# Routed rows of the first expert pair from a one-hot matmul, and the slots of the later pairs moved behind it, in a two-layer decoder trunk

## The chip, the cores and the metric

The kernel runs on one core of one Trainium2 chip. The metric is the device time of one execution in microseconds, as the median of several runs. Engines are called TensorE (PE in the profile, its weight loads PEld), VectorE (DVE), ScalarE (ACT), GpSimd (POOL) and SyncE (SP, which issues the weight DMAs).

## What is computed

A trunk of two layers over 256 tokens of width 1024, with 16 meta tokens ahead of them in layer 0 (272 tokens). Layer 0 has an mLSTM mixer, layer 1 a forgetting attention; each is followed by a mixture of experts, and that is what the change touches:

```python
def hier_moe(h, ...):
    top_g = jnp.argmax(gl, axis=-1)                      # one of 4 groups
    top_v, top_i = lax.top_k(el_g, TOP_K_IN_GROUP)       # 2 of its 4 experts
    p_e = jax.nn.softmax(top_v, axis=-1) * p_g
    gates = (one_hot(eidx, N_EXPERTS) * p_e[..., None]).sum(1)
    for grp in range(N_GROUPS):
        hg = jnp.einsum('td,edf->tef', x, w_gate[sl])
        hu = jnp.einsum('td,edf->tef', x, w_up[sl])
        act = jax.nn.silu(hg) * hu * gates[:, sl, None]
        y = y + jnp.einsum('tef,efd->td', act, w_down[sl])
    return y
```

16 experts of width 256. Everything is float32 but for small exact one-hot and counting matmuls in bf16.

## The kernel before, in words

Each expert has 64 slots (`CAP`), so that a pair of experts has 128, and there are 8 pairs (`NPAIR`). A token takes one slot at each of its two experts. Tokens lie in tiles: two of 128 rows and, in layer 0 only, a third of 16 rows (the meta tokens), `tiles_of(l)`.

*Routing* (`route`, L831 on VectorE). The normed rows of the stream are written by ScalarE to `tok` in SBUF (L575) and from there to `xs` in HBM (L579). VectorE works out groups, experts and, with counting matmuls (L1349), the slots: `tok4[:, 0:2]`, ready at L888. `one_hot` (L893) compares slots with the numbers of 256 slots at a time, in bf16, 12 operations in layer 0 and 8 in layer 1, into `sel`. `rows_of_slots` on TensorE (L1358) multiplies those by token numbers, one column for each block of 128 slots, and `row_of_slot` (L828) turns the result into the indices `idx`. GpSimd gathers with them, from `xs` into one of three buffers `xg` (L454): pair b waits for its part of `idx` and, from the fourth pair on, for the transposes that read the buffer last.

Beside it the weights: VectorE completes `tok4` (L902 to L905), TensorE transposes it (L1367), VectorE copies it to `row4` (L909), TensorE broadcasts its four rows over all partitions (L1371, operand `sel4` of 4 rows), ScalarE copies the result to `bc4` (L600), and `combine_weights` (L931 to L935) makes the combining matrix of a pair from it.

*The loop over pairs.* For each pair TensorE transposes the gathered rows in two halves of four blocks through bank 0 (`rows_to_cols`, L1384), evacuated by VectorE (`x_evac`, L923) and ScalarE (`xgT_evac`, L608); `gate_up(b)` (L1402) multiplies with the gate and up weights of both experts, each operand 64 columns wide, two side by side; silu on ScalarE (L616) and a product on VectorE (`act_mul`, L942) make `ha`; `act_tr` (L1409) transposes it, `down` (L1426) and `combine` (L1441 in layer 0, L1445 in layer 1) finish. The order on TensorE is written out: gate_up(b), [for b = 0: rows_of_slots for pairs 4 to 7], down(b-1), rows_to_cols(b+1, 0), act_tr(b), combine(b-1, 0), rows_to_cols(b+1, 1), combine(b-1, 1). Before the loop stand: rows_of_slots for pairs 0 and 1, for pairs 2 and 3, the transposes of tok4, the broadcast, rows_to_cols(0, 0) and (0, 1).

Every engine runs its own list in order; semaphores tie them. SyncE loads weights in a ring of 12 units of 1 MiB, six for each pair: gate and up of pair b+2 may be issued when gate_up(b) is done, its downs when down(b) is done (L307), in that order in one queue.

Of the kernel before, what the change touches and what calls it, by code (L numbers as in the profile page):

```python
# [7 lines left out]
ALU = mybir.AluOpType  # L8
ACT = mybir.ActivationFunctionType
# [31 lines left out]
def build(nc, io, out):  # L41
    ctx = ExitStack()
    with ctx:
# [54 lines left out]
        comb = big[:, NY * D:NY * D + NPAIR * NT].rearrange("p (b t) -> p b t", t=NT)  # L98
        sel = big[:, 0:6 * 256].bitcast(BF16).rearrange("p (c t s) -> p c t s", c=2, t=3)
# [141 lines left out]
        def wait_bank(pe, kind, ph, j):  # L241
            if before(kind, ph) + j >= 2:
# [8 lines left out]
                  "at_read": 8, "comb_ready": 8, "c_done": 64, "x_in0": 48, "x_in1": 48, "x_in2": 32}  # L251
# [131 lines left out]
        def _(pool):  # L383
# [63 lines left out]
            def moe(l):  # L447
                tiles, n, off = tiles_of(l)
                pool.wait_ge(*in_layer("xs_written", l, 16 * len(tiles)))
                for b in range(NPAIR):  # L450
                    pool.wait_ge(*in_layer("idx_ready", l, min(b // 2, 2) + 1))
                    if b >= NXG:
                        pool.wait_ge(*in_layer("tx_done", l, 2 * (b - NXG) + 2))
                    pool.indirect_dma_start(  # L454
                        out=xg[b % NXG], out_offset=None, in_=xs[l],
                        in_offset=bass.IndirectOffsetOnAxis(ap=idx[:, b:b + 1], axis=0)) \
                        .then_inc(sem(f"x_in{b % NXG}"), 16)
# [24 lines left out]
        def _(act):  # L482
# [75 lines left out]
            def moe(l):  # L558
# [39 lines left out]
                for r in range(4):  # L598
                    act.wait_ge(*in_layer("bc_mm", l, r + 1))
                    act.activation(bc4[:, r, 0:n], bank[4 + r][:, 0:n], ACT.Copy).then_inc(sem("bc_ready"), 1)  # L600

# [93 lines left out]
        def _(dve):  # L695
# [135 lines left out]
            def route(l):  # L831
# [58 lines left out]
                def one_hot(c0, base):  # L890
                    for c in (0, 1):
                        for t, rows, _ in tiles:
                            ins = dve.tensor_scalar(sel[0:rows, c, t, c0:c0 + 256], iota_f[0:rows, :], float(base),  # L893
                                                    tok4[0:rows, c, t:t + 1], ALU.add, ALU.is_equal)
                    ins.then_inc(sem("sel_ready"), 1)

                one_hot(0, 0)
                one_hot(256, 256)
                row_of_slot(l, 0, 0, 2, 1)

                dve.wait_ge(*in_layer("v_exp", l, 1))
                link(dve.tensor_scalar(dnn, exn, 1.0, None, ALU.add))  # L902
                link(dve.reciprocal(dnn, dnn))
                link(dve.tensor_tensor(tok4[:, 2, 0:nt].unsqueeze(2), dnn, pgn, ALU.mult))
                dve.tensor_tensor(tok4[:, 3, 0:nt].unsqueeze(2), tok4[:, 2, 0:nt].unsqueeze(2), exn, ALU.mult) \  # L905
                    .then_inc(sem("tok4_ready"), 1)
                row_of_slot(l, 1, 2, 4, 2)
                dve.wait_ge(*in_layer("row4_mm", l, 1))
                dve.tensor_copy(row4[:, 0:n], bank[3][0:MH, 0:n]).then_inc(sem("row4_ready"), 1)  # L909
                one_hot(0, 512)  # L910
                one_hot(256, 768)

            def moe(l):
# [3 lines left out]
                route(l)  # L917

# [39 lines left out]
                def add_combined(b):  # L958
                    for i in range(8):
# [212 lines left out]
        def _(pe):  # L1172
# [147 lines left out]
            def moe(l):  # L1320
# [41 lines left out]
                pe.wait_ge(*in_layer("xr_read", l, 1))  # L1362
                rows_of_slots(1, 0, (0, 1))
                rows_of_slots(2, 1, (2, 3))
                pe.wait_ge(*in_layer("tok4_ready", l, 1))
                for t, rows, c0 in tiles:
                    ins = pe.transpose(bank[3][0:4, c0 - off:c0 - off + rows], tok4[0:rows, :, t], ident[0:rows, 0:rows])  # L1367
                ins.then_inc(sem("row4_mm"), 1)
                pe.wait_ge(*in_layer("row4_ready", l, 1))
                for r in range(4):  # L1370
                    pe.matmul(bank[4 + r][:, 0:n], sel4[:, r, :], row4[:, 0:n], start=True, stop=True) \  # L1371
                        .then_inc(sem("bc_mm"), 1)

                def rows_to_cols(b, half):
                    if half == 0:
                        pe.wait_ge(*in_layer(f"x_in{b % NXG}", l, 16 * (b // NXG + 1)))
                        if b >= 1:
                            pe.wait_ge(*in_layer("xT_read", l, b))
                        else:
                            pe.wait_ge(*in_layer("idx_ready", l, 1))  # L1380
# [6 lines left out]
                def gate_up(b):  # L1387
# [4 lines left out]
                    else:  # L1392
                        pe.wait_ge(*in_layer("idx_ready", l, 2))
# [262 lines left out]
```

## Time and profile before

| | us |
|---|---|
| median of 3 runs | 719.53 (717.13 to 720.36) |
| the profiled execution, its own time | 722.15 |
| its span, first to last instruction | 720.4 |
| mean granted clock of TensorE | 0.926 |

Busy shares of the engines, and the span in 40 slices of 18 us:

```profile
PE 654.7 (91%) x2930; PEld 399.1 (55%) x2930; DVE 201.6 (28%) x628; ACT 138.5 (19%) x394; POOL 29.8 (4%) x56
PE   6899999885995889999998999999999579999994
PEclk9898999855998699999999999999999679999998
DMA  9995334100133369999999533140422447999931
```

How to read it: the first line is busy time, share of the span and instructions of each engine. In the other lines each digit is one slice in tenths; PEclk is the clock that TensorE was granted, where 1.0 is 2.4 GHz and 0.5 is 1.2 GHz. The experts of layer 0 begin in slice 13 (from 234 us), those of layer 1 in slice 32 (from 576 us); the routing stands just ahead of each, where the digits of PE and PEclk dip. In lists of instructions "out<-in", then the shapes as partitions x elements; "x32" is a number of instructions. A float32 matmul stands in the lists as two MATMULs, a transpose as one.

### The profile page before, as it was taken

Reading aid. Unit: us, or ns where it says so; the run is one execution under the profiler, and the core shown is the slowest. Engines: PE = TensorE matmul, PEld = TensorE weight load, DVE = VectorE, ACT = ScalarE, POOL = GpSimd, SP = SyncE. Lnnn points to the kernel's source line nnn. Section 1 sums busy time; section 2 is a strip of 40 time slices with the busy share of each in tenths; the row PEclk is TensorE's granted clock in tenths of the full one; section 3 lists DMA queues with packets and bytes.
Section 4 is the critical chain, followed back from the end, with each engine's and each line's share of the span. In section 5 each row is a group of like instructions: output and inputs, shape, how many; then the busy total and the mean of one; then the engine's idle time right before and its main releaser. Section 6 shows DMA issues by size and latency. Waiting matters only on the chain.

```text
span 720.4 us, 7665 instructions
## 1 busy us (share of the span) xinstructions
PE 654.7 (91%) x2930; PEld 399.1 (55%) x2930; DVE 201.6 (28%) x628; ACT 138.5 (19%) x394; POOL 29.8 (4%) x56
## 2 busy tenths in 40 slices
PE   6899999885995889999998999999999579999994
PEld 3686888442764335544445777777766334334331
DVE  2223100114005414444345232322410521112221
ACT  2102120221003111111123333333410411111110
POOL 4000000000000200000000100000000210000000
PEclk9898999855998699999999999999999679999998
DMA  9995334100133369999999533140422447999931
GB/s 286 256 286 186 117 117 162 71 0 1 58 117 121 116 263 370 408 419 422 401 348 289 183 116 117 59 170 6 176 70 110 159 184 298 409 422 421 418 137 60
DMA packets 59255, 150.03 MB, mean 208 GB/s; under 512 B 10224, under 2 KB 43056, under 8 KB 46928
## 3 DMA queue, kind: packets, MB, share of 16 engines
q1 hardware_dynamic: 55696, 136.71, 51.5%
q0 software_dynamic: 2912, 10.64, 4.4%
q10 hardware_dynamic: 608, 2.16, 0.8%
q8 instruction: 25, 0.41, 0.2%
q14 instruction: 14, 0.11, 0.1%
HBM read 146.27 MB, written 3.23 MB: 208 GB/s over the span
## 4 chain that ended last, share of the span: by engine, by line
PE 83%; DMA 6%; DVE 6%; issue 2%; ACT 2%; SPq 1%; ACTq 0%; DVEq 0%
PE bank L1182 33%; PE bank L1402 15%; PE bank L1426 7%; DMA ring<-in_moe_w_up 5%; PE bank L1441 3%; PE bank L1292 3%; PE bank L1445 3%; PE bank L1384 2%; PE bank L1191 1%; PE bank L1315 1%; PE bank L1563 1%; PE bank L1550 1%; PE bank L1371 1%; PE bank L1317 1%; PE bank L1224 1%
## 5 line engine op out<-in xcount | busy, mean ns | idle before, releaser
L1182 PE MATMUL bank<-xT,ring 128*128 128x272 f32 x768 | 190.7, 406 | 2.4 <-DVE xT L727 1.7
L1182 PEld LDWEIGHTS bank<-xT,ring 128*128 128x128 f32 x768 | 149.2, 197 | 37.4 <-issue 6.7
L1402 PE MATMUL bank<-ring,gate_area 128*64 128x512 f32 x512 | 120.5, 626 | 8.4 <-DMA ring<-in_moe_w_up 3.3
L1402 PEld LDWEIGHTS bank<-ring,gate_area 128*64 128x64 f32 x512 | 40.1, 144 | 82.9 <-issue 82.9
L1426 PE MATMUL bank<-ring,gate_area 128*64 128x512 f32 x256 | 57.9, 593 | 0.0
L942 DVE TENSOR_TENSOR qk_area<-qk_area,bank 128x256 f32<-128x256 f32 x16 | 6.7, 418 | 116.9 <-ACT qk_area L616 116.9
L1426 PEld LDWEIGHTS bank<-ring,gate_area 128*64 128x64 f32 x256 | 19.5, 137 | 35.3 <-issue 35.3
L454 POOL DMA_INDIRECT qk_area<-xs,idx x16 | 17.9, 1117 | 489.0 <-DVE idx L828 363.9
L1441 PE MATMUL bank<-big 128*128 128x272 f32 x128 | 32.5, 399 | 1.2 <-DVE big L956 1.2
L499 ACT ACTIVATE colT<-hT 128x272 f32<-128x272 f32 (+1 forms) x32 | 13.5, 425 | 96.1 <-DVE hT L823 78.1
L1445 PE MATMUL bank<-big 128*128 128x512 f32 x64 | 30.6, 606 | 1.2 <-DVE big L956 1.2
L616 ACT ACTIVATE qk_area<-bank 128x256 f32<-128x256 f32 x16 | 6.1, 383 | 131.5 <-PE bank L1402 131.5
L1182 PE MATMUL bank<-tok,ring 128*128 128x256 f32 x128 | 29.9, 385 | 0.5 <-DVE tok L1166 0.5
L961 DVE TENSOR_TENSOR hT<-hT,bank 128x272 f32<-128x272 f32 x64 | 27.8, 438 | 4.9 <-PE bank L1441 4.1
L1182 PE MATMUL bank<-big,ring 128*128 128x256 f32 x128 | 28.9, 379 | 0.0
L1384 PEld LDWEIGHTS bank<-ident,qk_area 128*128 128x128 f32 x128 | 18.4, 195 | 17.4 <-issue 12.6
L1182 PEld LDWEIGHTS bank<-tok,ring 128*128 128x128 f32 x128 | 23.6, 190 | 6.1 <-issue 2.5
L1441 PEld LDWEIGHTS bank<-big 128*128 128x128 f32 x128 | 23.2, 190 | 6.7 <-DVE big L956 2.2
L608 ACT ACTIVATE gate_area<-bank,gains_x 128x128 f32<-128x128 f32 x64 | 18.2, 368 | 43.9 <-PE bank L1384 43.9
L1292 PE MATMUL bank<-big,tok 128*128 128x257 f32 (+2 forms) x48 | 22.5, 605 | 4.2 <-DVE tok L789 4.2
L1182 PEld LDWEIGHTS bank<-big,ring 128*128 128x128 f32 x128 | 24.3, 190 | 3.5
L1384 PE MATMUL bank<-ident,qk_area 128*128 128x128 f32 x128 | 23.1, 307 | 1.8 <-DVE gate_area L923 1.6
(255 smaller groups left out, 564.7 us busy)
## 6 DMA issues: line engine op xcount, KB each, us to landing
ring<-in_moe_w_gate SPq DMA_DIRECT2D x32, 1024.0 KB, 11.8
ring<-in_moe_w_up SPq DMA_DIRECT2D x32, 1024.0 KB, 13.8
ring<-in_moe_w_down SPq DMA_DIRECT2D x32, 1024.0 KB, 7.2
ring<-in_m_w_in SPq DMA_DIRECT2D x12, 1024.0 KB, 11.6
ring<-in_kv_w SPq DMA_DIRECT2D x8, 1024.0 KB, 11.8
ring<-in_m_w_out SPq DMA_DIRECT2D x4, 1024.0 KB, 10.7
ring<-in_f_w_q SPq DMA_DIRECT2D x4, 1024.0 KB, 11.9
ring<-in_f_w_o SPq DMA_DIRECT2D x4, 1024.0 KB, 5.1
```

The lines of the kernel that those rows point to most:

```text
L454: pool.indirect_dma_start(out=xg[b % NXG], out_offset=None, in_=xs[l], in_offset=bass.IndirectOffsetOnAxis(ap=idx[:, b:b + 1], axis=0)) \
L499: act.activation(colT[k % 2][:, 0:n], hT[:, k, c0:c0 + n], ACT.Square).then_inc(sem(f"sq_{name}"), 1)
L608: ins = act.activation(xgT[b % 2][:, q, :], bank[0][:, (q - 4) * P:(q - 3) * P], ACT.Copy, scale=gains_x[:, l, q:q + 1])
L961: dve.tensor_tensor(hT[:, i, :], hT[:, i, :], bank[4 + i % 4][:, 0:NT], ALU.add) \
L1182: ins = pe.matmul(bank[c % 2][:, 0:n], w[:, k, half * P:half * P + P], x[:, k, 0:n], start=(k == 0), stop=(k == KB - 1))
L1191: pe.matmul(bank[b][:, 0:n], ones_f[:, :], colT[k % 2][:, 0:n], start=(k == 0), stop=(k == KB - 1)) \
L1292: ins = pe.matmul(bank[t][0:rows, 0:MDV + 1], stile[0:kr, c:c + rows], v0[0:kr, st, hd, :], start=(n_ == 0), stop=(n_ == len(srcs[t]) - 1))
L1384: ins = pe.transpose(bank[0][:, i * P:(i + 1) * P], xg[b % NXG][:, 4 * half + i:D:KB], ident[:, :])
L1402: ins = pe.matmul(bank[1][s, :], xgT[b % 2][:, q, s], ring[:, r:r + 2, q * FE:(q + 1) * FE], start=(q == 0), stop=(q == KB - 1))
L1426: ins = pe.matmul(bank[2 + half][s, :], haT[b % 2][:, f, s], unit_down(us[par])[:, f, half * HALF:(half + 1) * HALF], start=(f == 0), stop ...
L1441: ins = pe.matmul(bank[4 + i % 4][:, 0:n], y[:, i * P:(i + 1) * P], comb[:, b, 0:n], start=True, stop=True)
L1445: ins = pe.matmul(bank[4 + i][:, :], comb[:, b, t * P:(t + 1) * P], y[:, half * HALF:(half + 1) * HALF], start=(b == 0), stop=(b == NPAIR ...
```

## The change

The rows of pair 0 are no longer gathered. VectorE makes a float32 one-hot matrix `sel0` of the tokens against the first 128 slots (an equality for a token's first slot, then a second one added), and TensorE multiplies the rows in `tok` with it (`pick_rows`, two halves of four column blocks, over the tiles of the layer), which gives the transposed rows of pair 0 in bank 0 at once: it stands in for the gather and for rows_to_cols(0, ...). GpSimd's loop of gathers starts at pair 1.

The bf16 one-hots for slots 128 to 511 follow `sel0` on VectorE; the indices of pairs 1 and 2, 3 are found between the two halves of `pick_rows`. The rest of `tok4`, the one-hots for slots 512 to 1023 and the copies of the counts come after x_evac(0). The transposes of `tok4` and the broadcast (`slots_to_rows`) come after gate_up(0) on TensorE, with the copy to `row4` on VectorE ahead of act_mul(0) and the copies to `bc4` on ScalarE behind silu(0). combine_weights(0) and (1) come after the first round of the loop.

```diff
@@ GpSimd, moe
-                for b in range(NPAIR):
+                for b in range(1, NPAIR):
@@ ScalarE, moe: moved from ahead of xgT_evac(0)
                     silu(b)
+                    if b == 0:
+                        for r in range(4):
+                            act.wait_ge(*in_layer("bc_mm", l, r + 1))
+                            act.activation(bc4[:, r, 0:n], bank[4 + r][:, 0:n], ACT.Copy).then_inc(sem("bc_ready"), 1)
@@ VectorE, end of route (one_hot, row_of_slot, tok4, row4 leave it)
+                for t, rows, _ in tiles:
+                    ins = dve.tensor_scalar(sel0[0:rows, t, :], iota_f[0:rows, 0:P], tok4[0:rows, 0, t:t + 1], None,
+                                            ALU.is_equal)
+                link(ins)
+                for t, rows, _ in tiles:
+                    ins = dve.scalar_tensor_tensor(sel0[0:rows, t, :], iota_f[0:rows, 0:P], tok4[0:rows, 1, t:t + 1],
+                                                   sel0[0:rows, t, :], ALU.is_equal, ALU.add)
+                ins.then_inc(sem("sel0_ready"), 1)
@@ VectorE, moe, ahead of the loop
+                one_hot(P, 256, 0)
+                one_hot(256, 512, 256)
                 x_evac(0)
-                combine_weights(0)
-                combine_weights(1)
+                row_of_slot(l, 1, 1, 2, 1)
+                row_of_slot(l, 3, 2, 4, 2)
...
+                one_hot(0, 256, 512)
+                one_hot(256, 512, 768)
                 dve.tensor_copy(posc[:, 0:nt * NE], bank[2][:, 0:nt * NE])
...
+                dve.wait_ge(*in_layer("row4_mm", l, 1))
+                dve.tensor_copy(row4[:, 0:n], bank[3][0:MH, 0:n]).then_inc(sem("row4_ready"), 1)
+                act_mul(0)
                 row_of_slot(l, 3, 4, 8, 3)
...
                 for b in range(NPAIR):
-                    if b >= 2:
+                    if b == 1:
+                        combine_weights(0)
+                    if b >= 1:
                         combine_weights(b)
-                    act_mul(b)
+                        act_mul(b)
@@ TensorE, moe
+                def pick_rows(half):
+                    if half == 0:
+                        pe.wait_ge(*in_layer("xr_read", l, 1))
+                        pe.wait_ge(*in_layer("sel0_ready", l, 1))
+                    else:
+                        pe.wait_ge(*in_layer("xT_read0", l, 1))
+                    for i in range(4):
+                        for m, (t, rows, _) in enumerate(tiles):
+                            ins = pe.matmul(bank[0][:, i * P:(i + 1) * P], tok[0:rows, t, 4 * half + i:D:KB],
+                                            sel0[0:rows, t, :], start=(m == 0), stop=(m == nt - 1))
+                    ins.then_inc(sem("tx_done"), 1)
...
-                rows_to_cols(0, 0)
-                rows_to_cols(0, 1)
+                pick_rows(0)
+                rows_of_slots(1, 1, (1,))
+                rows_of_slots(2, 3, (2, 3))
+                pick_rows(1)
                 for b in range(NPAIR):
                     gate_up(b)
                     if b == 0:
+                        slots_to_rows()
                         rows_of_slots(4, 3, (4, 5, 6, 7))
```

In `pe.matmul(out, stationary, moving)` the second argument is the operand that is loaded as weights; `slots_to_rows` holds the transposes of tok4 (L1365 to L1368) and the broadcast (L1369 to L1372) unchanged.

## Rows read from the trace of the kernel before

**Rows 1.** The page, shares of the chain that ended last by engine.
```profile
PE 83%; DMA 6%; DVE 6%; issue 2%; ACT 2%; SPq 1%; ACTq 0%; DVEq 0%
```
**Rows 2.** The chain around the routing of layer 0: start us, us, what.
```profile
229.63 3.24 DVE big L893 x12
...
232.92 1.10 PE bank L1358 x12
234.02 0.65 PE bank L1367 x3
...
235.18 3.99 PE bank L1371 x8
...
240.25 0.70 DVE gate_area L923
...
241.00 1.12 PE bank L1384 x4
242.12 1.28 issue
243.39 9.37 PE bank L1402 x32
```
**Rows 3.** The whole chain, its pieces in layer 1, and two rounds of pairs.
```profile
258.50 8.64 PE bank L1402 x32
...
567.17 2.19 DVE big L893 x8
571.24 3.78 PE bank L1371 x8
...
579.25 8.70 PE bank L1402 x32
...
592.26 8.79 PE bank L1402 x32
...
609.40 7.02 PE bank L1402 x32
```
**Rows 4.** Stretches: us, busy (x) of PE, PEld, DVE, ACT, POOL, granted clock, DMA share, GB/s.
```profile
147.90:154.30 6.40, 6.40 (x12) 2.77 (x12) 0.00 (x0) 0.00 (x0) 0.00 (x0) 0.50 0.00 0
154.30:156.90 2.60, 2.60 (x7) 1.30 (x6) 0.27 (x3) 2.20 (x9) 0.00 (x0) 0.50 0.00 0
171.95:178.60 6.65, 6.65 (x24) 3.68 (x24) 3.51 (x7) 0.00 (x0) 0.00 (x0) 0.50 0.01 2
...
227.60:235.10 7.50, 3.62 (x36) 2.60 (x35) 5.43 (x25) 1.10 (x1) 1.22 (x1) 0.50 0.07 12
...
243.40:248.00 4.60, 4.60 (x12) 1.61 (x14) 0.76 (x3) 0.00 (x0) 0.41 (x1) 0.50 0.36 114
```
**Rows 5.** Lines L1384 and L1328: ns min/median/max, first and last start, forms.
```profile
L1384 PEld LDWEIGHTS bank<-ident,qk_area x128: 185/190/231, 239.1 to 686.6; 128*128 128x128 f32 x128
L1384 PE MATMUL bank<-ident,qk_area x128: 272/277/479, 239.1 to 686.7; 128*128 128x128 f32 x128
...
L1328 PEld LDWEIGHTS bank<-ident,hT x40: 90/140/143, 220.0 to 560.5; 128*128 128x128 f32 x32, 128*16 128x16 f32 x8
```
**Rows 6.** Weight loads of L1292 in order of time: start us, us, what.
```profile
150.19 0.50 PEld L1292 LDWEIGHTS bank<-big,tok 16*128 16x128 f32 x2 [0.65 <-issue]
151.34 1.35 PEld L1292 LDWEIGHTS bank<-big,tok 128*128 128x128 f32 x4 [0.66 <-issue]
153.36 0.12 PEld L1292 LDWEIGHTS bank<-big,tok 16*16 16x16 f32 x2 [0.66 <-issue]
```
**Rows 7.** Order of time: one VectorE operation of combine_weights, and L1358 in layer 1.
```profile
242.39 0.50 DVE L931 SCALAR_TENSOR_TENSOR gate_area<-gate_area,s_cols 128x272 f32<-128x272 f32 x1
...
568.46 0.35 PE L1358 MATMUL bank<-tcol,big 128*128 128x1 bf16 x8 [2.43 <-DVE big L893]
```
**Rows 8.** SyncE's issues of two downs, and landing times of the gathers (L454).
```profile
270.61 0.80 SPq L307 DMA_DIRECT2D ring<-in_moe_w_down  x2
...
DMA to landing us min/median/max: 4.5/7.7/9.8
```

More of the change, by code:

```diff
@@ L98, in build @@
         comb = big[:, NY * D:NY * D + NPAIR * NT].rearrange("p (b t) -> p b t", t=NT)
+        sel0 = big[:, 6 * 256:6 * 256 + 3 * P].rearrange("p (t s) -> p t s", t=3)
         sel = big[:, 0:6 * 256].bitcast(BF16).rearrange("p (c t s) -> p c t s", c=2, t=3)
@@ L250, in build @@
                   "sel_ready": 4, "idx_mm": 3, "tok4_ready": 1, "row4_mm": 1, "row4_ready": 1, "at_done": 8,
-                  "at_read": 8, "comb_ready": 8, "c_done": 64, "x_in0": 48, "x_in1": 48, "x_in2": 32}
+                  "at_read": 8, "comb_ready": 8, "c_done": 64, "sel0_ready": 1, "x_in0": 32, "x_in1": 48, "x_in2": 32}
         def in_layer(name, l, n):
@@ L597, in moe @@
                 act.preload_act_table(ACT.Silu)
-                for r in range(4):
-                    act.wait_ge(*in_layer("bc_mm", l, r + 1))
-                    act.activation(bc4[:, r, 0:n], bank[4 + r][:, 0:n], ACT.Copy).then_inc(sem("bc_ready"), 1)
                 def xgT_evac(b):
@@ L888, in route @@
                 link(dve.tensor_reduce(tok4[:, 0:2, 0:nt], t16[:, :, 0:nt, :], AX.X, ALU.add))
[L890 to L911, printed above, removed]
+                for t, rows, _ in tiles:
[6 more added lines that the diff above has]
+                ins.then_inc(sem("sel0_ready"), 1)
             def moe(l):
@@ L917, in moe, with one_hot @@
                 route(l)
+                def one_hot(c0, c1, base):
+                    for c in (0, 1):
+                        for t, rows, _ in tiles:
+                            ins = dve.tensor_scalar(sel[0:rows, c, t, c0:c1], iota_f[0:rows, c0 % 256:c0 % 256 + c1 - c0],
+                                                    float(base), tok4[0:rows, c, t:t + 1], ALU.add, ALU.is_equal)
+                    ins.then_inc(sem("sel_ready"), 1)
                 def x_evac(b):
@@ L962, in add_combined @@
                             .then_inc(sem("hadd0"), 1)
+                one_hot(P, 256, 0)
+                one_hot(256, 512, 256)
                 x_evac(0)
-                combine_weights(0)
-                combine_weights(1)
+                row_of_slot(l, 1, 1, 2, 1)
+                row_of_slot(l, 3, 2, 4, 2)
+                dnn, exn, pgn = [a[:, 0:nt, :] for a in (dn, ex, pg)]
+                dve.wait_ge(*in_layer("v_exp", l, 1))
+                link(dve.tensor_scalar(dnn, exn, 1.0, None, ALU.add))
+                link(dve.reciprocal(dnn, dnn))
+                link(dve.tensor_tensor(tok4[:, 2, 0:nt].unsqueeze(2), dnn, pgn, ALU.mult))
+                dve.tensor_tensor(tok4[:, 3, 0:nt].unsqueeze(2), tok4[:, 2, 0:nt].unsqueeze(2), exn, ALU.mult) \
+                    .then_inc(sem("tok4_ready"), 1)
+                one_hot(0, 256, 512)
+                one_hot(256, 512, 768)
                 dve.tensor_copy(posc[:, 0:nt * NE], bank[2][:, 0:nt * NE])
@@ L1360, in rows_of_slots @@
                     ins.then_inc(sem("idx_mm"), 1)
[L1362 to L1369, printed above, removed]
@@ L1370, in moe @@
-                for r in range(4):
-                    pe.matmul(bank[4 + r][:, 0:n], sel4[:, r, :], row4[:, 0:n], start=True, stop=True) \
-                        .then_inc(sem("bc_mm"), 1)
+                def pick_rows(half):
[9 more added lines that the diff above has]
+                    ins.then_inc(sem("tx_done"), 1)
@@ new lines, in slots_to_rows @@
+                def slots_to_rows():
+                    pe.wait_ge(*in_layer("tok4_ready", l, 1))
+                    for t, rows, c0 in tiles:
+                        ins = pe.transpose(bank[3][0:4, c0 - off:c0 - off + rows], tok4[0:rows, :, t],
+                                           ident[0:rows, 0:rows])
+                    ins.then_inc(sem("row4_mm"), 1)
+                    pe.wait_ge(*in_layer("row4_ready", l, 1))
+                    for r in range(4):
+                        pe.matmul(bank[4 + r][:, 0:n], sel4[:, r, :], row4[:, 0:n], start=True, stop=True) \
+                            .then_inc(sem("bc_mm"), 1)
@@ L1374, in rows_to_cols @@
                 def rows_to_cols(b, half):
                     if half == 0:
[L1376 to L1380, printed above, removed]
+                        pe.wait_ge(*in_layer(f"x_in{b % NXG}", l, 16 * (b // NXG + (b % NXG > 0))))
+                        pe.wait_ge(*in_layer("xT_read", l, b))
@@ L1392, in gate_up @@
                     else:
-                        pe.wait_ge(*in_layer("idx_ready", l, 2))
+                        pe.wait_ge(*in_layer("idx_ready", l, 1))
                     us = [expert_units(l, b, par) for par in (0, 1)]
```

## The prediction

> **What bounds the kernel now.** I first read the shares of the chain that ended last: 83% of it is TensorE and 6% DMA [rows 1]. So a removed wait counts only if TensorE stood behind it on that chain, and work that is added to TensorE counts in full unless it fills such a wait. Next I read the pieces of that chain around the routing of layer 0 [rows 2]. From the slots (VectorE L888, ends at 229.6 us) to the first gate matmul (L1402, 243.39) lie 13.8 us: one-hots 3.24, the matmuls that find rows 1.10, transposes and a copy up to 235.18, four broadcast matmuls 3.99, two sets of transposes with their evacuations, 1.28 of issue. The gather itself is almost hidden. It lands while the broadcast runs, and the piece after L1371 is already L1384. So what the gather covers today (broadcast and its round trip) is not free once it is taken away: it goes somewhere. Layer 1 has the same picture with two tiles in place of three [rows 3]. After that every pair costs TensorE a fixed round, so a shift of the second pair's gate matmuls (258.50 and 592.26) [rows 3] reaches the end one to one. Its weights ask for nothing else: the downs of pair 2 are issued at 270.61, behind down(0), and move with it [rows 8].
>
> I therefore make the sum for one quantity per layer: the start of gate_up(1), in three terms: start of gate_up(0), its length, and the gap up to gate_up(1).
>
> **Layer 0, start of gate_up(0).** Removed from the chain: both one_hots of 256 columns ahead of the first PE work, the transposes, copy and broadcast, two row transposes. Added on VectorE: three equality operations of 128 columns and three that add. Twelve of 256 columns took 3.24 us, so 0.27 each and 0.135 for half; an operation of the second kind took 0.50 for 272 columns [rows 7], so at most 0.25. With two links that is 3 x 0.135 + 3 x 0.25 + 0.15 = 1.3, and TensorE begins at 229.63 + 1.3 = 231.0.
>
> Added on TensorE: pick_rows twice. Each is 4 column blocks x 3 tiles, in f32, and f32 matmuls stand in the trace as two passes (L1371 has 8 records for 4 calls), so 24 passes of 128 columns. One such pass at half clock is 0.21: four transposes take 1.12, the last with 0.48 of its own latency [rows 2, 5], (1.12 - 0.48) / 3. That makes 5.1. The clock is at half here: it reads 0.50 from 227.6 on, before the first pick, and still under the first gate matmuls [rows 4].
>
> To this comes a cost that the diff hides. The third tile has 16 rows, so the height of the operand changes from 128 to 16 and back in each block, 7 changes per call. The trace prices it in L1292, whose matmuls mix the two heights: two passes of 257 columns followed by a change take 151.34 - 150.19 = 1.15 us; four passes with one change take 153.36 - 151.34 = 2.02, so two without change take 0.87 and a change takes 0.28 at half clock [rows 6]. A second row agrees: finding rows costs 1.10 for 12 matmuls with mixed heights, and 0.35 for 8 with one height [rows 2, 7], which is twice as much for each. 7 x 0.28 = 1.9. Bounds: 5.1 (no change costs) to 7.1. I take 7.0, since L1292 is f32, two passes, and just this mix.
>
> So pick_rows(0) runs from 231.0 to 238.0. The one_hots that follow on VectorE (6 x 0.135 and 6 x 0.27) end at about 233.4, under it, and cost nothing. The 18 one-column matmuls for pairs 1 to 3 take 18 x 0.09 = 1.65, up to 239.7; the evacuation of the first half (0.70 on VectorE, L923 in rows 2) lies beside them. pick_rows(1): up to 246.7. From the end of today's last transposes (241.00 + 1.12) to L1402 are 1.27 us [rows 2], and that stays. gate_up(0) starts at 247.9: **4.5 us later** than today, 0.7 later at the low bound.
>
> **Its length.** Today 9.37 us, of which 4.6 at half clock [rows 2, 4]; a full-speed one takes 7.02 [rows 3]. I leave it unchanged in the main case (see the first rival).
>
> **The gap.** Moved into it, behind the last gate matmul: transposes and copy, 235.18 - 234.02 = 1.16 today and about 1.1 at full clock, then 8 broadcast passes, half of 3.99, so 1.9. Nothing covers them: act_tr(0) and the second half of pair 1's transposes are queued behind them on TensorE, and gate_up(1) waits for those. Against that, ha is ready sooner (VectorE runs act_mul(0) right after its copy), which saves about 0.3. ScalarE's four bc copies run beside the broadcast. VectorE now runs combine_weights(0) and (1) ahead of act_mul(1): six operations of about 0.5 [rows 7] beside a gate_up of 7 us, hidden. Net **+2.7** (bounds +2.4 and +3.0). **Layer 0: 4.5 + 2.7 = +7.2 us.**
>
> The gathers of the later pairs: POOL waits for `idx_ready` 1 as before, which now comes after x_evac(0), at about 239; three gathers follow, each landing 4.5 to 9.8 us after its issue [rows 8], so pair 1's is there by about 250, and TensorE wants it at about 262. Hidden, with 10 us to spare. Gather 3 waits for the second pick instead of the second transposes. SP: the weights of pair 2 are issued at the end of gate_up(0), 17 us ahead of use.
>
> **Layer 1.** Two tiles of 128 rows, so 16 passes and no change of height. VectorE: 2 x 0.135 + 2 x 0.25 + 0.15 = 0.9, TensorE begins at 568.1. Pick: 16 x 0.21 = 3.4, up to 571.5. Rows: 12 x 0.045 = 0.5, but x_evac (0.70 and two hand-overs) ends last, 572.3. Second pick up to 575.7, and 1.27 more: 577.0 against 579.25, so **-2.3**. The gap: +1.1 + 1.9 - 0.4 = **+2.6**. Layer 1: **+0.3** (bounds 0 and +0.6).
>
> **Sum:** +7.5 us. The profiled execution has 722.15 (span 720.4), 2.6 above the median of 719.53; I add the shift to the median: **727.0 us**.
>
> **A rule of the Trainium skill weighed.** The picks read `tok` as the stationary operand with a step of 8 f32 numbers. Today's transposes of `qk_area` do the same, and their weight loads last 190 ns at the median against 140 for the unstrided ones of `hT` [rows 5]; both stay below the 0.21 of a half-clock pass, so I charge nothing. "SBUF — State Buffer" (Door 1: The DMA port swizzle) says that f32 reads which step past a 16-byte line pay a penalty; by it, as an estimate, 24 loads in layer 0 and 16 in layer 1 with the measured 50 ns more, twice each, would add 4.0 and make it 731.0. The trace has the longer load, and four strided transposes in 1.12 us, no longer spacing than half clock explains.
>
> **Rivals.**
> 1. *The clock rises under the picks in both layers.* Today's stretch before gate_up(0) is transposes, one-column matmuls and a broadcast whose operand has 4 rows; the clock stays at 0.50 through it. It also stayed at 0.50 through 6.65 us of pure transposes, and rose only after 4.6 us of gate matmuls [rows 4]. Picks are full multiplications. "TensorE: Matmul & The Clock Gate" (Part 4: PE-mode transpose) says that transposes do not count as busy for the clock; the 0.50 under pure transposes agrees. Price if it rises after some 4 us of picking: in layer 0 the rest of the first pick gains about 1.1, the second 3.4 (half of 7.0, less the rest of the change cost), gate_up(0) 9.37 - 7.02 = 2.35: together 6.9. In layer 1: 1.7 on the second pick, 8.70 - 7.02 = 1.7 on gate_up(0): 3.4. Total 7.5 - 10.3 = -2.8, 716.7 us: the other side, not slower. It decides from the point where the clock rises before pick_rows(1). Against it: the clock also stayed at 0.50 through 9.0 us without a break in L1292 and the scores after it (6.40 and 2.60) [rows 4], real multiplications of which half have 16 rows. The picks of layer 0 have the same mix and the same breaks. Chance 0.12.
> 2. *The clock rises in layer 1 alone,* where every operand is full height: 7.5 - 3.4 = +4.1, 723.6 us. For it: nothing of L1292's kind is in the way. Against it: each burst is only 3.4 us with 0.8 between, shorter than the 4.6 that the gate matmuls needed. Chance 0.22.
> 3. *The change of height costs nothing in a pick,* because narrow passes hide it: 2 x 1.9 = 3.8 less, 723.2 us. Against: rows 6. Chance 0.12. Together with rival 2: 719.8, chance 0.06.
> 4. *Pair 1 waits for its gather,* or the cold start of gate_up(1) lasts longer since the gap without full multiplications is longer (today gate_up(1) takes 8.64 us in place of 7.02 for that reason [rows 3]): up to 3 us more, 730. Chance 0.04 by itself; it widens the main case upwards.
>
> **How the numbers follow.** Main case (clock stays down, changes cost): 0.44, 725 to 731. The range of 8 in 10 takes in rivals 2 and 3 and most of their sum, and leaves out the bottom of rival 1: 718 to 731. A difference of 0.5% is 3.6 us, about what a measurement of this kernel can tell: slower means above 723.1. Slower: 0.44 + 0.04 + more than half of rivals 2 and 3 (0.17) = 0.65. Faster (below 715.9): the lower tail of rival 1, 0.06. The rest, 0.29, within.
>
> **What would show each step.** In layer 0 the picks would stand as two groups of 24 matmuls `bank<-tok,big` with 7 us each, weight loads of the 16-row tile with gaps of 0.2 to 0.3 beside them, the granted clock at 0.50 from 231 to beyond 248, gate_up(0) at about 248 and 9 us long, then L1371's passes behind it and gate_up(1) at about 265.7. In layer 1 gate_up(0) at 2.3 before today's place relative to the routing, and the gap about 6.9 instead of 4.3. The prediction is wrong if the clock reads 1.00 during pick_rows(1), if a pick of layer 0 takes about 5, or if the gap does not grow.

## The result, and the profile after

| | before | changed |
|---|---|---|
| median | 719.94 us (717.13 to 724.14, 4 runs) | 734.13 us (733.69 to 734.65, 4 runs) |
| ratio, 95% interval | | 1.0198 (1.0168 to 1.0228) |
| the profiled execution, its own time (span) | 722.15 (720.4) | 734.47 (732.7) |
| mean granted clock | 0.926 | 0.920 |

The changed kernel is slower, as forecast, but by 14.2 us in place of 7.5, and 734.1 lies outside the range of 718 to 731. In the profiled executions the difference is 12.3. The other 1.9 is that the profiled execution of before was 2.2 above its median and that of the changed kernel 0.3. What favoured the other executions of before is not shown. The traces of the runs do show how much can differ ahead of every edit: the first one-hot of layer 0 starts between 224.04 us (no16) and 229.63 (before), and it starts later the longer the granted clock stood at 0.50 in the first 71 us: 3.4 us in no16, 10.2 in contig, early and picks_all (starts at 226.6 to 226.9), 13.6 or 13.7 in before, changed, group16 and early2 (228.9 to 229.6). So the pieces below are counted from the first one-hot of their layer.

The page of the changed kernel, busy shares and the chain that ended last by engine:

```profile
PE 670.5 (92%) x2984; PEld 413.3 (56%) x2984; DVE 203.7 (28%) x638; ACT 138.7 (19%) x394; POOL 26.2 (4%) x54
...
PE 84%; DMA 6%; DVE 5%; issue 2%; ACT 1%; SPq 1%; ACTq 0%; DVEq 0%
```

TensorE is busy 15.8 us longer and still the chain [rows 1]. The pieces of the chain around the routing of layer 0 answer to [rows 2] (start us, us, what; L1382 is pick_rows, L1369 rows_of_slots, L1390 and L1395 tok4's transposes and the broadcast, L1405 rows_to_cols, L1423 gate_up):

```profile
229.11 0.68 DVE big L893 x3
...
229.81 0.87 DVE big L897 x3
...
230.82 8.15 PE bank L1382 x24
238.97 1.56 PE bank L1369 x18
240.53 8.07 PE bank L1382 x24
248.60 1.28 issue
249.88 9.23 PE bank L1423 x32
259.11 0.43 PE bank L1390 x3
...
259.56 0.44 DVE colT L977
...
260.05 2.10 PE bank L1395 x8
262.14 1.93 PE bank L1369 x24
...
265.58 1.12 PE bank L1405 x4
...
267.98 8.72 PE bank L1423 x32
```

The gather is gone from the chain, and the two picks (8.15 and 8.07) stand in the place of everything that [rows 2] had between the one-hots and the gate matmuls. The gap behind gate_up(0) is a queue on TensorE until 264.1, broken only by the copy on VectorE (0.44). Layer 1, which answers to [rows 3]:

```profile
576.85 0.49 DVE big L893 x2
...
577.37 0.62 DVE big L897 x2
...
578.12 4.09 PE bank L1382 x16
...
582.98 4.18 PE bank L1382 x16
587.16 1.28 issue
588.44 8.91 PE bank L1423 x32
...
604.45 9.44 PE bank L1423 x32
```

The same three terms as in the prediction, from the starts in these chains. The start of gate_up(0) is counted from the first one-hot of its layer (229.63 and 567.17 before, 229.11 and 576.85 after):

| us, after minus before | predicted | measured | from |
|---|---|---|---|
| layer 0, start of gate_up(0) | +4.5 | +7.0 | 20.77 - 13.76 |
| its length | 0 | -0.1 | 9.23 - 9.37 |
| gap to gate_up(1) | +2.7 | +3.1 | 8.87 - 5.74 |
| length of gate_up(1) | 0 | +0.1 | 8.72 - 8.64 |
| layer 1, start of gate_up(0) | -2.3 | -0.5 | 11.59 - 12.08 |
| its length | 0 | +0.2 | 8.91 - 8.70 |
| gap to gate_up(1) | +2.6 | +2.8 | 7.10 - 4.31 |
| length of gate_up(1) | 0 | +0.65 | 9.44 - 8.79 |
| sum | +7.5 | +13.2 | |

The rest up to 12.3 is -0.5 ahead of the routing of layer 0 (its first one-hot begins sooner by that) and about -0.4 in the remainder. So the miss sits mostly in the two starts: 2.5 and 1.8 of 5.7 us.

### The profile page after: what moved, and what is told of

Same layout as the page of the kernel before. It is cut to its first block, busy times and chain, and to the rows that moved or that the text cites. A ratio compares the mean times of both kernels' runs of the same rounds, so it can differ in the third digit from the quotient of the medians.

```text
span 732.7 us, 7779 instructions
## 1 busy us (share of the span) xinstructions
PE 670.5 (92%) x2984; PEld 413.3 (56%) x2984; DVE 203.7 (28%) x638; ACT 138.7 (19%) x394; POOL 26.2 (4%) x54
## 4 chain that ended last, share of the span: by engine, by line
PE 84%; DMA 6%; DVE 5%; issue 2%; ACT 1%; SPq 1%; ACTq 0%; DVEq 0%
PE bank L1193 33%; PE bank L1423 15%; PE bank L1447 7%; DMA ring<-in_moe_w_up 5%; PE bank L1382 3%; PE bank L1462 3%; PE bank L1303 3%; PE bank L1466 3%; PE bank L1405 1%; PE bank L1202 1%; PE bank L1326 1%; PE bank L1587 1%; PE bank L1574 1%; PE bank L1328 1%; PE bank L1235 1%
## 5 line engine op out<-in xcount | busy, mean ns | idle before, releaser
L1423 PE MATMUL bank<-ring,gate_area 128*64 128x512 f32 x512 | 121.3, 629 | 8.1 <-issue 5.1
L1423 PEld LDWEIGHTS bank<-ring,gate_area 128*64 128x64 f32 x512 | 39.9, 145 | 83.8 <-issue 83.8
L455 POOL DMA_INDIRECT qk_area<-xs,idx x14 | 14.1, 1010 | 505.2 <-DVE idx L829 374.4
L1382 PE MATMUL bank<-big,tok 128*128 128x128 f32 (+1 forms) x80 | 24.5, 472 | 5.9 <-DVE big L897 5.4
L1382 PEld LDWEIGHTS bank<-big,tok 128*128 128x128 f32 (+1 forms) x80 | 20.4, 330 | 9.2 <-issue 8.6
## 6 DMA issues: line engine op xcount, KB each, us to landing
ring<-in_f_w_q SPq DMA_DIRECT2D x4, 1024.0 KB, 12.3
```

The source lines that it names most:

```text
L455: pool.indirect_dma_start(out=xg[b % NXG], out_offset=None, in_=xs[l], in_offset=bass.IndirectOffsetOnAxis(ap=idx[:, b:b + 1], axis=0)) \
L1382: ins = pe.matmul(bank[0][:, i * P:(i + 1) * P], tok[0:rows, t, 4 * half + i:D:KB], sel0[0:rows, t, :], start=(m == 0), stop=(m == nt - 1))
L1423: ins = pe.matmul(bank[1][s, :], xgT[b % 2][:, q, s], ring[:, r:r + 2, q * FE:(q + 1) * FE], start=(q == 0), stop=(q == KB - 1))
```

## The experiments

### What paces a pick

The prediction gave a pass of a pick 0.21 us at half clock and a change of operand height 0.28. Layer 0 took 8.15 for 24 passes with 7 changes, layer 1 4.09 for 16 passes with none: 0.256 each. My theory now: a weight load that steps by 8 numbers sets the pace, whatever the clock. The rival: any float32 load of 128 columns costs that for so narrow a pass.

**contig** stores the rows in `tok` with their columns in block order, so that the picks and the row transposes read with step 1:

```diff
-                        ins = act.activation(tok[0:rows, t, half * HALF:(half + 1) * HALF], b[0:rows, :], ACT.Copy,
-                                             scale=rs[0:rows, t:t + 1])
+                        by_q = tok[0:rows, t, :].rearrange("p (q a) -> p q a", q=KB)
+                        ins = act.activation(by_q[:, :, half * (P // 2):(half + 1) * (P // 2)],
+                                             b[0:rows, :].rearrange("p (a q) -> p q a", q=KB), ACT.Copy,
+                                             scale=rs[0:rows, t:t + 1])
...
-                            ins = pe.matmul(bank[0][:, i * P:(i + 1) * P], tok[0:rows, t, 4 * half + i:D:KB],
+                            ins = pe.matmul(bank[0][:, i * P:(i + 1) * P], tok[0:rows, t, (4 * half + i) * P:(4 * half + i + 1) * P],
```

> The changed kernel with one difference: ScalarE stores the rows in tok (and so xs and xg) with the columns ordered as the blocks want them, so that every operand of pick_rows and rows_to_cols is read with step 1 in place of step 8. Theory S (the weight load with a step of 8 numbers takes 0.26 us for a pass and sets the pace, whatever the clock): layer 0 picks fall from 8.15 to about 7.1 each, layer 1 picks from 4.1 and 4.2 to 3.4 each at half clock and less where the clock is up; in all 3.5 to 6 us less than the changed kernel, 728 to 730.5 us. Theory F (any float32 load of 128 columns for a pass of 128 takes 0.26): the picks stay at 8.1 and 4.1, 734 us. If the reordered copy costs ScalarE much, the routing starts later by that; it shows in L576.

Measured: 729.46 us (728.45 to 733.32), ratio to before 1.0160 (1.0115 to 1.0204); its interval overlaps that of the changed kernel, so the verdict rests on the trace. The picks at half clock fell less than expected: 7.54 and 7.50 in layer 0, 3.77 for the first one of layer 1. Stretches of it, in the columns of [rows 4]: first and second pick of layer 1, gate_up(0) of layer 1, and last the first pick of layer 0.

```profile
575.54:579.30 3.76, 3.76 (x23) 3.70 (x24) 1.69 (x8) 0.11 (x1) 0.00 (x0) 0.50 0.00 0
580.08:582.10 2.02, 2.02 (x16) 1.85 (x16) 1.92 (x11) 0.00 (x0) 1.10 (x1) 1.00 0.00 0
583.41:590.40 6.99, 6.99 (x32) 2.60 (x32) 0.16 (x2) 0.00 (x0) 0.94 (x1) 1.00 0.61 209
228.34:235.80 7.46, 7.46 (x24) 5.67 (x24) 2.60 (x12) 0.00 (x0) 0.00 (x0) 0.50 0.01 2
```

And the same two picks of layer 1 in the changed kernel (578.12 and 582.98, with the end of the second one apart):

```profile
578.12:581.90 3.78, 3.77 (x16) 3.78 (x17) 1.70 (x8) 0.11 (x1) 0.00 (x0) 0.50 0.00 0
582.98:585.30 2.32, 2.32 (x10) 2.32 (x10) 2.22 (x12) 0.00 (x0) 1.23 (x2) 1.00 0.00 0
585.40:587.10 1.70, 1.70 (x7) 1.46 (x7) 1.08 (x5) 0.00 (x0) 0.74 (x1) 0.50 0.74 255
```

This separates them. With step 1 the second pick runs at full clock in 2.05 us, 0.128 for a pass, and gate_up(0) behind it takes 7.09. With step 8 it took 4.18, 10 passes in 2.32 us at a granted clock of 1.00: twice the clock brings nothing, PEld is busy without a gap, and under it the clock fell back to 0.50 at 585.3, so that gate_up(0) started cold (8.91). At half clock the step costs little (8.15 against 7.54 in layer 0, 0.256 against 0.236 for a pass in layer 1): there even a pass with step 1 is slower than the 0.21 that I had charged. The row transposes are read with step 1 too here. Their weight loads lasted 141 ns at the median in place of 190, and four of them still took 1.12 us at half clock, as in the changed kernel (263.33 here, 265.58 there): from transposes the price of the step could not be read. "SBUF — State Buffer" (Door 1: The DMA port swizzle) of the Trainium skill says that f32 accesses which step past a 16-byte line pay a penalty; the two second picks agree with it.

That the step also brings the clock down is not shown. gate_up(0) of layer 1 took 7.09 in both kernels whose picks have step 1 (contig, picks_all) and 8.46 to 8.91 in four with step 8 (changed, group16, no16, picks_clock), but 7.09 in pick_only, which has step 8.

**group16** puts the 16-row tile's matmuls last in each pick, so that the height changes once per call, not 7 times:

```diff
-                    for i in range(4):
-                        for m, (t, rows, _) in enumerate(tiles):
+                    for i, m in [(i, m) for i in range(4) for m in (0, 1)] + [(i, 2) for i in range(4) if nt == 3]:
+                        for t, rows, _ in (tiles[m],):
...
-                                            sel0[0:rows, t, :], start=(m == 0), stop=(m == nt - 1))
+                                            sel0[0:rows, t, :], start=(i == 0 and m == 0), stop=(m == nt - 1),
+                                            skip_group_check=True)
```

> The changed kernel with the matmuls of the 16-row tile put behind all those of the 128-row tiles in each pick, one change of operand height per call in place of 7. Theory H (each change costs 0.28 us at half clock): picks of layer 0 fall by 6 x 0.28 = 1.7 each to 6.5, in all 3.4 us less than the changed kernel, 730.7; layer 1 unchanged. Rival (the 16-row tile costs as such, or changes are hidden): 734.

Measured: 730.45 us, ratio 1.0145 (1.0107 to 1.0183), again an interval that overlaps that of the changed kernel. Its chain:

```profile
230.62 6.39 PE bank L1382 x24
237.02 1.56 PE bank L1369 x18
238.58 6.30 PE bank L1382 x24
```

1.76 and 1.77 less for six changes, 0.29 each: the price that the prediction read from [rows 6], to 0.01.

**no16** leaves the 16-row tile out of the picks: `enumerate(tiles[:2])` in place of `enumerate(tiles)`, `stop=(m == 1)`.

> Leaves out of pick_rows the tile of the 16 meta tokens in layer 0, so their rows are missing from pair 0. Theory H with S: a pick of layer 0 is 16 passes of 0.26 = 4.2 like one of layer 1, 3.9 less than 8.1: 8 passes are 2.1 of it, 7 changes 1.9 (0.26 each). All: 7.8 us less than the changed kernel, 726.3.

Measured: picks of 4.08 and 4.11, as layer 1's; one time of 723.17. That is 3.1 less than expected, and its routing started 5.1 sooner than that of the changed kernel, ahead of the edit (224.04 against 229.11). So the tile with 16 of 272 tokens makes up half of each pick of layer 0: 2.05 for its 8 passes and 2.0 for the changes.

### Is it the half clock that makes the picks slow?

Rival 1 of the prediction had the clock rise under the picks. **picks_clock** starts them at full clock:

```diff
+                def warm(times):
+                    for i in range(times):
+                        pe.matmul(bank[3][:, 0:n], ones_f[:, :], hT[:, i % KB, off:NT], start=True, stop=True)
...
+                pe.wait_ge(*in_layer("gl_sub", l, 1))
+                warm(7 if l == 0 else 8)
...
                 ins.then_inc(sem("pos_mm"), 1)
+                warm(5 if l == 0 else 4)
```

> The changed kernel with matmuls of hT that nobody reads ahead of the picks, so that these start at full clock. Theory S (weight loads with a step of 8 set a pass at 0.26 whatever the clock): picks of layer 0 fall only by the cheaper changes, 8.15 to 7.5, those of layer 1 stay at 4.1, and gate_up(0) gains up to 2 where the clock holds through the picks: 729 to 732. Rival 1 of the prediction (half clock is what makes the picks slow): 4.0 for each pick of layer 0 and 1.7 in layer 1, 720 or less.

Measured: 732.95 us (731.64 to 735.05), ratio 1.0171 (1.0136 to 1.0206). Its picks of layer 0, the first one in two stretches, and last the first pick of layer 1:

```profile
231.25:234.30 3.05, 3.05 (x11) 2.69 (x11) 2.60 (x12) 0.00 (x0) 0.00 (x0) 1.00 0.03 5
234.40:239.00 4.60, 4.60 (x14) 3.49 (x14) 0.00 (x0) 0.00 (x0) 0.00 (x0) 0.50 0.00 0
240.64:248.70 8.06, 8.06 (x24) 6.20 (x24) 4.41 (x19) 0.00 (x0) 2.19 (x2) 0.50 0.38 130
578.87:582.90 4.03, 4.03 (x23) 4.02 (x24) 1.69 (x8) 0.00 (x0) 0.00 (x0) 1.00 0.00 0
```

The first pick started at 1.00 and still took 7.82, the second 8.07; the clock went down under the first one. The first pick of layer 1 had 1.00 from end to end and took 4.06, against 4.09 in the changed kernel, where it was 0.50 but for the last 0.3 us. So a pick with step 8 gains nothing by the full clock, and the half clock is not what makes it slow. gate_up(0), which was to gain up to 2 us, took 9.46 and 8.84: no gain, as the clock was down again before it.

What brings the clock down under the picks stays open. "TensorE: Matmul & The Clock Gate" (Part 4: PE-mode transpose) of the Trainium skill says that transposes do not count as busy for the clock; the picks are multiplications, and it fell under them too. It also fell under picks with step 1 (at 234.6 in picks_all, below) and there at 241.4, 1.2 us into gate_up(0). And it can rise under picks with step 8: at 229.1 in no16, at 581.9 in the changed kernel.

### The two halves of the change

**move_only** is the kernel before with the broadcast, its transposes and copy behind gate_up(0), the gather kept:

```diff
-                pe.wait_ge(*in_layer("tok4_ready", l, 1))
-                for t, rows, c0 in tiles:
...
                     if b == 0:
+                        slots_to_rows()
+                        broadcast()
                         rows_of_slots(4, 3, (4, 5, 6, 7))
```

> The kernel before with one half of the change: tok4's transposes, the copy and the broadcast moved behind gate_up(0), combine_weights(0) and (1) moved with them; gather of pair 0 and all one-hots as before. Theory G (the gather lands at 239 whatever stands before it, so taking the broadcast out of its shadow gains nothing ahead of gate_up(0) and costs the gap 3.1 us in layer 0 and 2.8 in layer 1): 5.9 us over the kernel before, about 725.8; the picks then account for the other half of the 12 to 14 us. Rival (the broadcast and not the gather held gate_up(0) back): gate_up(0) starts 3 us earlier and the sum is about 720.

Measured: 728.71 us (725.88 to 734.48), ratio 1.0118 (1.0068 to 1.0169). Layer 0 in its chain (L1389 rows_to_cols, L1407 gate_up, L1376 the broadcast):

```profile
233.64 4.82 DMA qk_area<-xs,idx
...
238.51 1.13 PE bank L1389 x4
...
242.80 9.57 PE bank L1407 x32
...
253.31 2.70 PE bank L1376 x8
...
262.32 10.05 PE bank L1407 x32
```

Now the gather's 4.82 us are open on the chain, where before the broadcast filled them, and gate_up(0) starts no sooner: 242.80 - 229.47 = 13.3 against 13.76. The gap grew from 5.74 to 9.95 and gate_up(1) from 8.64 to 10.05, more than the 3.1 that I expected, and the clock accounts for the rest (stretches of the gap and of the head of gate_up(1)):

```profile
252.40:254.60 2.20, 1.68 (x9) 1.15 (x8) 0.76 (x2) 0.85 (x3) 0.00 (x0) 1.00 0.48 97
254.70:262.30 7.60, 5.98 (x38) 4.14 (x37) 3.66 (x11) 2.17 (x7) 0.51 (x1) 0.50 1.01 426
262.32:268.30 5.98, 5.98 (x14) 1.87 (x16) 0.68 (x2) 0.00 (x0) 0.64 (x1) 0.50 0.54 201
```

The clock fell early in the gap, at 254.6, so part of the broadcast and the first 6.0 us of gate_up(1) ran at half. In the changed kernel it fell in the last part of the gap, at 264.5 of 259.1 to 268.0. The profile of move_only is that of its slowest execution (734.48), 5.8 above its median, so these pieces show more than its usual cost.

**pick_only** is the other half: picks, with tok4's transposes and the broadcast between them, ahead of gate_up(0):

```diff
                 pick_rows(0)
+                slots_to_rows()
                 rows_of_slots(1, 1, (1,))
+                pe.wait_ge(*in_layer("row4_ready", l, 1))
                 rows_of_slots(2, 3, (2, 3))
+                broadcast()
                 pick_rows(1)
```

> The other half of the change: pair 0 picked, but tok4's transposes, the copy and the broadcast ahead of gate_up(0) as before, here between the two picks; combine_weights(0) and (1) ahead of the loop as before. Nothing of the broadcast is in a gather's shadow now. Sum: layer 0 gate_up(0) at 231.0 + 8.1 + 0.7 + 1.6 + 4.0 + 8.1 + 1.3 = 254.8, 11.4 later than before, gap as before; layer 1 about 3.5 later: 15 us over the kernel before, 734, about the changed kernel itself. The two halves then add to more than the whole, because both pay for the same shadow. Rival (the move was the main cost): 728.

Measured: 735.10 us (731.86 to 737.57), ratio 1.0219 (1.0185 to 1.0253). gate_up(0) of layer 0 starts at 254.06, 25.3 after the first one-hot against 13.76 before; 11.4 more was expected, 11.55 came. By the ratios the halves cost 8.5 and 15.8 us of 720, 24 together, where the whole costs 14.2: each half alone loses the shadow in which the gather and the broadcast hid each other.

**picks_all** joins contig and group16 and puts the broadcast behind rows_to_cols(1, 1), into TensorE's wait for ScalarE (and ScalarE's copies to bc4 behind xgT_evac(1)):

```diff
                         rows_to_cols(b + 1, 1)
+                    if b == 0:
+                        broadcast()
```

> The changed kernel with three mends together: columns of tok in block order (step 1), the 16-row tile's matmuls last in each pick, and the broadcast behind rows_to_cols(1, 1), in TensorE's wait for ScalarE. Sum of the single prices: picks of layer 0 at 0.236 for a pass and one change, 5.9 each in place of 8.1 (4.4 less), layer 1 1.5 to 2.5 less and gate_up(0) there up to 1.8 less, the gaps 2 us less each: 10 to 12 us less than the changed kernel, 722 to 724, still not below the kernel before.

Measured: 720.38 us (718.98 to 723.50), ratio 1.0016 (0.9988 to 1.0043): no difference from the kernel before can be seen. Picks of layer 0 are 4.46 and 4.65 (the clock was up for part of each), those of layer 1 3.77 and 2.05. It was further down than expected: the picks of layer 0 took 4.5 in place of 5.9. The third mend did not do its part. Its gap in layer 0 (L1410 rows_to_cols, L1400 the broadcast, L1428 gate_up):

```profile
253.71 1.12 PE bank L1410 x4
254.83 3.92 PE bank L1400 x8
258.75 8.59 PE bank L1428 x32
```

TensorE's wait for ScalarE is 1.3 us long in the kernel before (257.24 to 258.50), and the broadcast at half clock takes 3.92, and 3.71 in layer 1. So it stands on the chain, and the gaps are 9.81 and 7.61, in place of 8.87 and 7.10 in the changed kernel and of the 2 us less that were expected. The gain is all in the picks and in gate_up(0). With these mends the cost of the change can no longer be seen in the times; in the traces the stretches from the first one-hot to the end of gate_up(1) are still 3.2 longer than before in layer 0 and 0.2 shorter in layer 1.

### A version that beats both

If gate_up(0) hangs on the gather, its index should come sooner and nothing else ahead of it. **early** is the kernel before with that order, the gather kept (GpSimd's waits follow it):

```diff
+                one_hot(0, P, 0)
+                dve.wait_ge(*in_layer("v_exp", l, 1))
...
+                row_of_slot(l, 0, 0, 1, 1)
+                dve.wait_ge(*in_layer("row4_mm", l, 1))
+                dve.tensor_copy(row4[:, 0:n], bank[3][0:MH, 0:n]).then_inc(sem("row4_ready"), 1)
+                one_hot(P, 256, 0)
+                one_hot(256, 512, 256)
...
                 rows_to_cols(0, 0)
+                rows_of_slots(2, 3, (1,), last=False)
                 rows_to_cols(0, 1)
+                rows_of_slots(3, 3, (2, 3))
```

> The kernel before, gather kept, with the index of pair 0 found first: one-hots of 128 slots, its matmuls and its index; the rest of tok4, its transposes and the broadcast then fill the gather's time, and the indices of pairs 1 to 3 are found in the two waits of rows_to_cols(0, .). Theory G (gate_up(0) hangs on the landing of the gather, 9.5 us after the slots, and its index can be ready 1.2 us sooner): gate_up(0) 1.2 to 1.7 us earlier in layer 0 and about 1 in layer 1, gap and clock as before: 717 us. Rival (the indices of pairs 1 to 3 in the waits push rows_to_cols or pair 1's gather): no gain.

Measured: 717.47 us (10 runs), ratio 0.9972 (0.9943 to 1.0001), at the edge of what can be told. gate_up(0) starts 12.0 after the first one-hot in layer 0 (238.94 - 226.90) and 12.4 in layer 1 (575.08 - 562.70), against 13.76 and 12.08: 1.7 sooner in layer 0, as expected, and 0.3 later in layer 1, where 1 us sooner was expected.

**early_clock** adds the matmuls of picks_clock to it, and three more ahead of rows_to_cols(0, 0).

> As the run early, with matmuls of hT that nobody reads put into the stretches in which TensorE waits (12 calls ahead of the one-hots, 3 ahead of rows_to_cols(0, 0)), to hold the clock up. Theory C (the half clock after the routing costs 2.35 us on gate_up(0) of layer 0 and 1.7 in layer 1, and twice 2 us on the broadcast, which is hidden): gate_up(0) takes 7.0 in both layers, 4 us less than the run early, 713. Rival (the clock falls anyway, or the added matmuls delay the chain): 717 or more.

Measured: 717.83 us, ratio 0.9985 (0.9962 to 1.0009), no gain over early, where 713 was expected. The clock stood at 1.00 under the broadcast's start and again from 235.2, but gate_up(0) of layer 0 still took 8.69, and 9.24 in layer 1: it fell at 238.6 and at 573.1, while transposes and one-column matmuls ran just ahead of gate_up(0). Full matmuls right up to gate_up(0) were not tried.

**early2** shortens the gap: the indices of pairs 4 to 7 are found in TensorE's waits of rows_to_cols(1, .) (VectorE turns them into `idx` behind the evacuation of act_tr(0)).

```diff
                     if b == 0:
-                        rows_of_slots(5, 3, (4, 5, 6, 7))
...
                     act_tr(b)
+                    if b == 0:
+                        rows_of_slots(5, 3, (4, 5), last=False)
...
                         rows_to_cols(b + 1, 1)
+                    if b == 0:
+                        rows_of_slots(5, 3, (6, 7))
```

> As the run early, and the indices of pairs 4 to 7 are found in TensorE's two waits of rows_to_cols(1, .) in place of right behind gate_up(0). Theory G (the gap is TensorE's own queue: 24 one-column matmuls of mixed height are 1.93 us of it in layer 0 and 16 of one height 0.5 in layer 1, while TensorE idles about 0.7 and 1.3 for the evacuations): the gap falls from 5.74 to about 4.0 in layer 0 and from 4.3 to 3.9 in layer 1, and the clock has less time to fall: 2 to 4 us less than the run early, 714 to 715. Rival (the pieces spill over the waits): 717.

Measured: **714.99 us** (11 runs), ratio to the kernel before 0.9942 (0.9916 to 0.9968). It beats both kernels, the one before by 0.6%; against early the intervals overlap. Its chain in layer 0 (L1358 rows_of_slots, L1384 rows_to_cols, L1402 gate_up):

```profile
239.96 0.92 PE bank L1358 x12
...
241.24 10.08 PE bank L1402 x32
...
252.74 0.85 PE bank L1358 x12
253.60 0.64 PE bank L1384 x4
254.24 0.85 PE bank L1358 x12
...
255.52 7.09 PE bank L1402 x32
```

The gap is 4.20 in place of 5.74 (layer 1: 3.50 in place of 4.31), and gate_up(1) takes 7.09 in both layers: the clock stood at 1.00 through the gap. Over the runs, in their profiled executions:

| kernel | gap, gate_up(1) in layer 0 | in layer 1 |
|---|---|---|
| before | 5.74, 8.64 | 4.31, 8.79 |
| changed | 8.87, 8.72 | 7.10, 9.44 |
| move_only | 9.95, 10.05 | 7.46, 9.77 |
| early | 5.74, 9.90 | 4.31, 7.09 |
| early2 | 4.20, 7.09 | 3.50, 7.09 |

gate_up(1) takes 7.09 or 8.6 to 10.1, and the same gap can be followed by unlike lengths (8.64 and 9.90 behind 5.74, 8.79 and 7.09 behind 4.31), so a single profile does not price this term, and that the shorter gap is what held the clock up is not shown. Of the 5.9 us by which early2's two stretches from the first one-hot to the end of gate_up(1) are shorter than before, 3.25 are the length of gate_up(1) and 2.35 the gaps.

## Why the prediction was right or wrong

*Right in direction and in mechanism.* The gather was hidden by the broadcast, and removing it only exposed what stood in its shadow: move_only and pick_only show both sides. The height change is worth what [rows 6] gave (0.29 against 0.28 at half clock). The gap grew by 3.1 and 2.8, against 2.7 and 2.6: in layer 0 transposes, copy and broadcast came to 3.0 (259.11 to 262.14), as priced, and the 0.3 credited for the earlier ha did not appear (3.91 from the end of rows_of_slots to gate_up(1), against 3.81 before). The gathers of the later pairs stayed hidden, and so did the moved one-hots.

*Wrong: the term "one such pass at half clock is 0.21".* This is the step that failed. The term was read from transposes, which stand in the trace as one MATMUL; a pick's float32 matmul is two, and its passes took 0.256. Over 48 and 32 passes that is 2.2 + 1.5 of the 4.3 us by which the two starts missed the forecast. PEld was busy almost without a gap in the picks of layer 1 (3.78 of 3.78 us, and 3.70 of 3.76 in contig), so the weight load was the bound. The step of 8 is about half of the miss at half clock: with step 1 a pass still takes 0.236. The prediction saw the step, 190 ns against 140 in [rows 5], and dismissed it, as no longer spacing showed behind four transposes; contig shows that transposes do not show it. At full clock the step is all of it (0.256 against 0.128), and that was the state of a good part of the second pick of layer 1. The estimate by the rule of the Trainium skill ("SBUF — State Buffer", Door 1: The DMA port swizzle), 731.0, was nearer than the sum without it, but in part by luck: it charged the measured 50 ns for each of 80 passes, where the step costs 20 to 25 at half clock.

*Wrong: "0.135 for half" of a one-hot.* Three operations of 128 columns took 0.68 (0.23 each) and the second kind 0.87 (0.29): half the columns are far from half the time. From the first one-hot to the first pick are 1.71 us in layer 0 and 1.27 in layer 1, 0.4 and 0.35 above the forecast.

*Lengths left unchanged.* gate_up(0) kept its length within 0.2, as said. gate_up(1) was 0.1 and 0.65 longer. Rival 4 had named the longer gap without full multiplications, at 0.04; since this length differs by 1.3 and 1.7 between before and early behind equal gaps, whether the 0.65 is due to the gap is not shown.

*The rivals.* 1 and 2 needed the clock to rise under the picks and stay. In layer 1 it rose during the first one (581.9) and fell during the second (585.3). So one sign that the prediction had named against itself, 1.00 during pick_rows(1), did come there, for 2.3 us, but not the gain that was to come with it: picks_clock shows that the full clock does nothing for a pick with step 8. With step 1 it does: in picks_all the clock rose at 231.2 under the first pick of layer 0, and the two picks took 4.46 and 4.65. 3 is refuted by group16.

*The range* ended at 731: a pick had bounds of 5.1 and 7.1, and nothing above 0.21 for a pass, although the rule that was weighed gave 731.0 by itself.

## What to carry to other kernels

Before taking away a transfer, ask what its wait covers: here the broadcast sat in the gather's shadow, and either one, taken out, put the other on the path. Price a matmul by rows with the same number of passes and the same operand step: a pass whose weights are read with a step of 8 float32 numbers ran at the same pace at half and at full clock. Storing the rows in block order removed that, and ScalarE's copies took the same 678 ns with it. And fill TensorE's waits around an evacuation with the small matmuls that otherwise stand in its queue, but only with what fits: early2 moved one-column matmuls and its gap fell from 5.74 to 4.20, picks_all put 3.92 us of broadcast into a wait of 1.3 and its gap grew.

## What the runs showed of the hardware

- A float32 matmul of 128 stationary and 128 moving columns takes 2 x 0.256 us with a stationary step of 8 numbers, at 0.50 (changed kernel, layer 1) and at 1.00 granted clock (picks_clock, layer 1), and 2 x 0.128 at 1.00 with step 1 (0.236 each at 0.50, both contig).
- The weight load of a row transpose lasts 141 ns at the median with step 1 (contig) and 190 with step 8 (changed), and four transposes take 1.12 us at half clock either way.
- The granted clock can fall from 1.00 to 0.50 while TensorE is busy without a break: at 585.3 in the changed kernel and at 234.3 in picks_clock under picks with step 8, in picks_all at 234.6, 0.4 us into a pick with step 1, and at 241.4, 1.2 us into gate_up(0).
- A change of operand height between 128 and 16 rows costs 0.29 us at half clock (group16).
- In layer 0 VectorE one-hots of 128 columns cost 0.23 us each (changed, float32 out) or 0.21 (early, bf16 out), where 256 columns cost 0.27 (before, bf16 out).
